# One inference step of a hybrid decoder layer on one core: the stages in front of the experts run once over all tokens, or twice over half of them each

## What is computed

```python
h   = x * (1 + sc_m) + sh_m                    # x is layernormed, sc/sh/gate from c @ w_ada
p   = h @ w_in                                 # 1024 -> 4608 columns
xs  = ps + (prev - ps) * mu_shift              # ps: the first 1792 columns, prev: the row before
r, k, v, decay, a, g = ...                     # from xs
y, wkv = _rwkv7_scan(r, decay, k, v, kk, a)    # state 64x64 per head, 8 heads, token after token
A   = (groupnorm(y) + bonus) * g
B   = window attention of q, k, v              # last 128 keys and the block's own, 8 heads, sinks
mix = (sigmoid(ga) * (A @ w_pa) + sigmoid(gb) * (B @ w_pb)) @ w_o
x   = LN(alpha * x + gt_m * mix)
ff  = PEER(x * (1 + sc_f) + sh_f)              # 8 heads, 2 x 128 keys, 16 of 16384 experts each
x   = LN(alpha * x + gt_f * ff)
```

## Time and profile before

| what | us |
|---|---|
| two runs | 4090.26, 4094.36 |
| median | 4092.31 |
| span of the profiled execution | 4092.5 |
| front, up to the experts | 1588 |
| peer_up | 1218 |
| peer_down | 1286.5 |
| TensorE busy | 3521.5 (86%) |
| VectorE busy | 2376.5 (58%) |
| GpSimd busy | 1416.8 (35%) |
| ScalarE busy | 1092.1 (27%) |

### The profile page before, as it was taken

How to read it: one execution, slowest core, us unless ns; L and a number is a source line. 1 busy time by engine, 2 the same in 40 slices (tenths; PEclk the granted TensorE clock), 3 DMA queues, 4 the chain that set the end, 5 groups by cost and what they waited for, 6 DMA issues and landing times. The chain is left out here.

```text
span 4092.5 us, 58784 instructions
## 1 busy us (share of the span) xinstructions
PE 3521.5 (86%) x22506; PEld 2542.8 (62%) x22506; DVE 2376.5 (58%) x4792; ACT 1092.1 (27%) x1919; POOL 1416.8 (35%) x1269
## 2 busy tenths in 40 slices
PE   6998999997879999988889989886787788778996
PEld 3666666673666888766666667664555455555565
DVE  3364222225223433999979888985666666665345
ACT  2221111111322232322262446343111111111122
POOL 0001111110002011344455545453666566665540
PEclk8999999997779999999999999998899899999998
DMA  5111110105123134788899999899999999999992
GB/s 196 36 31 38 33 33 29 37 28 202 67 84 148 42 101 140 247 291 282 302 389 348 338 355 380 328 338 353 391 390 382 363 394 397 394 395 396 393 350 76
DMA packets 367137, 973.75 MB, mean 238 GB/s; under 512 B 36017, under 2 KB 133497, under 8 KB 359952
## 3 DMA queue, kind: packets, MB, share of 16 engines
q0 software_dynamic: 150912, 549.52, 35.2%
q1 hardware_dynamic: 215952, 420.45, 29.1%
HBM read 863.29 MB, written 106.55 MB: 237 GB/s over the span
## 5 line engine op out<-in xcount | busy, mean ns | idle before, releaser
L2107 POOL DMA_INDIRECT u_rows<-in_u_rows,idx_u x512 | 640.5, 1251 | 859.1 <-DVE dots L2145 689.4
L2145 DVE CUSTOM_DVE_ANT_0 u_rows<-u_rows,x_rows 128x1024 f32<-128x1024 f32 x512 | 620.1, 1222 | 130.9 <-DMA u_rows<-in_u_rows,idx_u 110.0
L2118 POOL DMA_INDIRECT v_rows<-in_v,idx_v x512 | 590.2, 1153 | 258.0 <-issue 141.1
L2627 PE MATMUL hid_ps<-dh,u_high 128*128 128x512 f32 x1152 | 475.3, 413 | 84.9 <-DVE u_low L2884 62.2
L2627 PE MATMUL hid_ps<-dl,u_high 128*128 128x512 f32 x1152 | 472.0, 410 | 0.0
L2627 PE MATMUL hid_ps<-dh,u_low 128*128 128x512 f32 x1152 | 469.4, 407 | 0.0
L3084 ACT ACTIVATE dh<-v_raw 128x1024 fp32r<-128x1024 f32 x128 | 135.3, 1057 | 720.4 <-DMA v_raw<-in_v 549.7
L2627 PEld LDWEIGHTS hid_ps<-dh,u_high 128*128 128x128 f32 x1152 | 225.1, 195 | 151.4 <-DVE u_low L2884 84.3
L2204 PE MATMUL ff_ps<-v_rows,diag 128*8 128x512 f32 x2048 | 260.1, 627 | 65.2 <-DMA v_rows<-in_v,idx_v 63.6
L3139 PE MATMUL turn_ps<-w_high,dh 128*128 128x512 f32 x384 | 172.3, 449 | 150.1 <-DVEq L3221 125.1
L723 PE MATMUL side_ps_scan<-h,w_side_scan 128*128 128x344 f32 x768 | 269.7, 477 | 1.4 <-DMA w_side_scan<-in_w_side 1.2
(11 more groups left out here) (458 smaller groups left out, 6533.3 us busy)
## 6 DMA issues: line engine op xcount, KB each, us to landing
u_raw<-in_u SPq DMA_DIRECT2D x128, 512.0 KB
v_raw<-in_v SPq DMA_DIRECT2D x128, 512.0 KB, 12.3
hidden_saved<-hid SPq DMA_DIRECT2D x128, 256.0 KB, 6.6
gates_saved<-gates SPq DMA_DIRECT2D x32, 1024.0 KB, 8.0
hidden_back<-hidden_saved SPq DMA_DIRECT2D x128, 256.0 KB, 13.8
g_back<-gates_saved SPq DMA_DIRECT2D x64, 320.0 KB, 14.1
g_back<-gates_saved SPq DMA_DIRECT2D x32, 384.0 KB, 20.6
side_saved<-side_scan SPq DMA_DIRECT2D x16, 516.0 KB
```

The source lines that it names most:

```text
L2107: self.nc.gpsimd.indirect_dma_start(self.u[:, n % RU], None, self.io["u_rows"], bass.IndirectOffsetOnAxis(ap=index, axis=axis)).then_inc(l ...
L2118: self.nc.gpsimd.indirect_dma_start(self.v[:, n % RV], None, self.io["v"], bass.IndirectOffsetOnAxis(ap=index, axis=0)).then_inc(self.v_la ...
L2145: V.tensor_tensor_reduce(self.u[:, n % RU], self.u[:, n % RU], self.xt[:], 1.0, 0.0, ALU.mult, ALU.add, accum_out=self.dots[:, i % 2, k:k ...
L2627: mm = nc.tensor.matmul(ps[b % 2][:], u[:, b % RING, k], h[:, k], start=at == 0, stop=at == 3 * KD - 1)
```

## The change

The front is run twice. Part A holds prompt tokens 0 to 511 and the 8 samples (520 tokens, two tiles of 260 columns), part B tokens 512 to 1023 (one tile of 512). The row of stages is inputs, scan, group norm (with the samples in A), attention (with the samples' in A), merge and output for A, and then all of it for B; nothing of B stands beside A. What B needs of A is carried: the scan's state, the last projected row, and the last 128 keys and values. Weights (w_in, the side blocks, w_o, the merge's, the gate's) are loaded by each part. A scan has 8 chunks, an attention 4 blocks.

```diff
+class Part:
+    def __init__(self, tag, at, ns, before):
+        self.tag, self.at, self.ns, self.before = tag, at, ns, before
+        self.tp = TP // 2
+        self.t = self.tp + ns
+        self.nt = 2 if ns else 1
+        self.tn = self.t // self.nt
...
+PART_A = Part("a", 0, NS, None)
+PART_B = Part("b", TP // 2 + NS, 0, PART_A)
...
-                    rwkv_inputs(**env)
-                    rwkv_scan(**env)
-                    rwkv_samples(**env)
-                env["early"] = Early(nc, sems, mix)
-                attention(**env)
...
-                merge(**env)
...
-                output_and_queries(**env)
+                rwkv_inputs(**env, part=PART_A, h=ha, w=w, w_loaded=w_loaded, x_stored=x_stored)
+                rwkv_scan(**env, part=PART_A, h=ha)
+                rwkv_samples(**env, part=PART_A, x_at=x_at)
+            env["early"] = Early(nc, sb, sems, first, PART_A)
+            attention(**env, part=PART_A, x_at=x_at)
+            output_and_queries(**env, ha=ha, x_at=x_at)
...
+                    rwkv_inputs(**env, part=PART_B, h=hb, w=w, w_loaded=w_loaded, x_stored=None)
+                    rwkv_scan(**env, part=PART_B, h=hb)
+                    rwkv_samples(**env, part=PART_B)
+                env["early"] = Early(nc, sb, sems, second, PART_B)
+                attention(**env, part=PART_B)
+                output_dense(**env)
```

```diff
+    side_at = SIDE_SCAN if part.ns else 0
+    sides = SIDE - side_at
...
-                for n in range(3, COUNT + SIDE_MOVED):
+                if part.ns:
+                    sp.dma_start(before[:], io["shift_before"]).then_inc(small_loaded, 16)
+                else:
+                    for n in range(3):
+                        load(n)
...
+                for n in range(3, COUNT + sides):
                     load(n)
...
-        PAUSES = (3, 1, 4, 2, 2, 2, 2, 2, 2, 2, 2)
-        assert sum(PAUSES) == NT * KD
+        PAUSES = (4, 1, 3, 4, 4, 4, 4, 2, 2, 2, 2)
+        assert sum(PAUSES) == 2 * 2 * KD
```

```diff
-                low(0)
-                low(1)
-                for j in range(len(TILES)):
-                    for n in range(KD):
-                        join(j, n)
-                        if j == 0 and n + 2 < KD:
-                            low(n + 2)
-                        if j and n == 2:
-                            centre(j - 1)
...
-                        if j and n == 5:
-                            scale(j - 1)
+                for n in range(KD):
+                    o.join(dve, n)
+                o.centre(dve, 0)
+                o.centre(dve, 1)
+                o.scale(dve, 0)
+                o.scale(dve, 1)
```

```diff
-    out += [("rows", 0), ("split_u", 0), ("low_u", 0), ("scores", 0, 0), ("query", 0, 1), ("load_u", 2), ("split_u", 1), ("low_u", 1)]
+    out += [("rows", 0), ("split_u", 0), ("low_u", 0), ("scores", 0, 0), ("scores", 0, 1), ("query", 0, 1),
+            ("load_u", 2), ("split_u", 1), ("low_u", 1)]
...
-                out.append(("scores", m + 1, 0))
-                out.append(("query", m + 1, 1))
+                out += [("scores", m + 1, 0), ("scores", m + 1, 1), ("query", m + 1, 1)]
...
-                out.append(("scores", m + 1, 1))
+                out += [("scores", m + 1, 2), ("scores", m + 1, 3)]
```

More of the change, by code:

```diff
@@ L914, in step @@
                         return
[L915 removed]
+                    multiply(pe, n, 0)
                     for l in range(NL):
@@ L950, in step @@
                         S.activation(rhs, seq_ps[:, 0], ACT.Copy, scale=-1.0).then_inc(rhs_ready, 1)
-                    for t in takes(0) if n is not None else ():
-                        side.take(act, n, t)
+                    if n is not None:
+                        take(act, n, 0)
                     for l in range(NL):
@@ L1138, in _ @@
                 pe.wait_ge(g2_loaded, 16)
+                if not part.ns:
+                    for p in range(NP):
+                        variance(p)
+                    for p in range(0, NP, 2):
+                        back(p)
+                        back(p + 1)
+                        gate(p)
+                        gate(p + 1)
+                    return
                 ada.product(pe, 0)
```

2214 lines of the change are left out of this document (1185 added, 1029 removed).

## The result

The changed kernel takes 4316.5 us (4312.07 and 4320.94) against 4092.31 us: ratio 1.055, 95% interval 1.052 to 1.0581. The profiled execution spans 4310.3 us against 4092.5, so 217.8 us are to be found. The forecast was 4338.

The account below looks back on a forecast made before the run. It took almost every stage of the first 1588 us as bound by TensorE or a chain of dependent steps. Terms 168 - 42 + 22 + 12 - 10 + 9 + 68 + 19 = +246 us gave 4338 us, range 4224 to 4425.

Parts of the forecast that it names:

- Inputs: Input stages of both parts: more side blocks on TensorE, the bounding engine, and doubled edges; +168 us.
- Scan: Scan stages: A's chunks stay near before's, B's shorten without side work; -42 us.
- I expect both clocks in turn and take 28: B's scan: TensorE's clock alternates, so a chunk takes 28 us, between 22.3 at full clock and 34.6 at low.
- rival 1: B's scan and attention: the clock stays full, giving 4224 us; chance 0.12.
- Group norm and samples: Group norm and sample stage: a chain that mostly doesn't shrink with tokens, 80 us for A, 36 for B; +22 us.
- Attention: Attention: blocks of 21 us at low clock and doubled ends, +12 us; loads moved to the next stage, -10.
- Merge: Merge stage: same matmul time, edges paid twice; +9 us.
- Output: Output stage: layernorm chains with nothing beside them, 36 us in each part; +68 us.
- Experts: Expert stages: first weights loaded later, +6 us, and scores in quarters through one PSUM bank, +12.
- rival 3: peer_up: quartered scores hold TensorE and VectorE 8 us per selection, some 60 us more, 4398 us; chance 0.05.
- rival 2: B's scan, attention and bare layernorm chains: the clock is low throughout, giving 4409 us; chance 0.09.
- rival 4: B's inputs: side blocks are free because VectorE's chain holds the stage, giving 4141 us; chance 0.04.

Follow-up runs that it names:

- experiment 1: The changed kernel with part B's side blocks in the inputs making one of their eight products; 4214.99 us, one run.
- experiment 2: The changed kernel with 16 of part B's side blocks put back into B's scan, 6 left in its inputs; 4261.9 us, ratio 1.0421.
- experiment 12: The kernel before with its scan's loop written out, and extra unused matmuls at attention's start and in its first and last block; 4046.24 us, ratio 0.9874.
- experiment 4: The changed kernel with 16 extra unused matmuls at the start of each part's attention and 9 more per block; 4265.43 us, ratio 1.043.
- experiment 3: The changed kernel with 16 extra unused matmuls only at the start of each part's attention; 4298.06 us, one run.
- experiment 5: The kernel before with peer_up's scores in four quarters through one PSUM bank instead of two halves through two; 4121.69 us, ratio 1.0072.
- experiment 11: The changed kernel with 20 extra unused matmuls in front of the first chunk of B's scan; 4324.65 us, ratio 1.0551.
- experiment 10: The changed kernel with B's scan written as a loop of two chunks per turn; 4298.74 us, one run.

## Why the prediction was right, and by which steps

The direction, the range and, to 22 us, the size held. By step:

- **Inputs (+168; measured +187.5).** The mechanism held and experiment 1 confirms it: 36 blocks in B, one behind the other on TensorE. Mis-sized were the block, 7.40 us where I took 7.0 (0.10 more of matmuls, 0.30 of gap; 36 x 0.4 = 14), and A by 7.6, of which its blocks, some 7.2 us of matmuls as taken, had no share. TensorE was busy 90% of A's stage and 92% of B's, not over 95%.
- **Scan (-42; measured -90.3): the step that failed in size.** It is the term "I expect both clocks in turn and take 28". The chain was right: 22.3 worked out, 22.4 measured. What replaced the 28 is 23.5 on average ((1464.2 - 1299.5) / 7), since the low clock held for one chunk and a bit and not in each; that is 36 of the 48 us. So it is more than a size: the change between both clocks in each chunk did not come, and a chunk of B at 22 was the prediction's own sign for rival 1. A gives 14 more (and before's scan, 2 us shorter than the 559 I took, takes 2 off): I gave it before's 34.6 per chunk and it took 33.0. The sentence that the side work costs 12.1 of its 14.2 was a wrong reading too, and the level worked out beside it, where 2.4 us cost 1.25, spoke against it: 9.4 is side work, 2.7 the loop (experiments 2, 12). With 9.4 I would have seen that the move from the scan to the inputs loses a third of those 14.2 us and not a seventh; the sum for the place was still right, because chunk B left the loop as well.
- **Group norm and samples (+22; +10.8).** Inside the bounds (+6 to +38); B's share was 28.5, and A's 75.5, where I took 36 and 80.
- **Attention (+12 - 10; +8.0).** The block of 21 us at the low clock was right (20.7), and so was its cause, the clock lost in blocks with nothing beside them: experiment 4 takes some 50 us out by filling the pauses, and experiment 3 shows that a warm start is not enough. The loads in front of the merge gave 3.4 back, 15.4 against 18.82, not 10.
- **Merge (+9; +12.7).** By my cut 8.9 of the 12.7 are the wait in front of the product with w_o (7.10 and 9.10 us, before 7.32), which the forecast had in the output stage. The merge's own share is 3.8, less than the 9.
- **Output (+68; +56.0, or +64.9 with those 8.9).** The two chains were 71.8 for 72. A's stage was 203.7 for 205, but the terms that I wrote down for A (46, 8, 36 and 92 to 108) give 182 to 198 and not 205. Measured they are 49.3 for the products without their start, 34.1 for the chain, 110.6 for the queries and 9.8 of waiting for B's first weights, so this closeness is partly luck. B was 87.2 for 98: the products 46.3 for 45, their start of 8 stands in the merge's row, and the split came within the 37.7 of the chain instead of 9 behind it.
- **Experts (+18; +30.1).** The direction was right, the waits of rival 3 are real but half of what it gave: 51.0 us over 18 of them, of which peer_up pays 32.1. My 1 to 1.5 us per selection was too little: experiment 5 measured 30 / 9 = 3.3 us. The path was in the prediction, a quarter that waits for the copy of the one before it, which itself waits in ScalarE's order, up to 8.2 us; its price of 1 to 1.5 us was worked out from no row.

The misses of the scan (-48) and of the inputs and experts (+20, +12) lie on opposite sides; that the sum came within 22 us is partly luck. Rival 1 was half true: the clock stayed full in most of B's scan, and not in attention. Rivals 2 and 4 fell. Part of rival 3 came.

The Trainium skill ("TensorE: Matmul & The Clock Gate", "A second HAM failure mode: psum-queue depth-cycling") describes a kernel in which short idle times between groups of matmuls, not long waits, are enough to send the clock back and forth. Attention agrees in that short idle times were enough, 2.47 and 1.11 us in front of scores and values, and differs in that the clock did not go back and forth but stayed at 0.50 throughout.

## What to carry to other kernels

- Work that fills the pauses of a chain is not free there, but price it at each place by two runs: the same 14.2 us cost 9.4 in the scan and 14.8 in a stage of dense matmuls. Moving it to "somewhere else" is a loss as long as that place is bound by the same engine.
- Splitting a kernel by tokens keeps the matmul time and doubles what doesn't shrink: bare chains between stages (72 us here), the ends and starts, and the three attention blocks that lost their companion and with it the clock.
- A loop costs what its edges take and what the clock does behind them, and the price is not carried from one stage to another: 2.7 us per chunk of 34.4 in before's scan, 1.2 of 33.0 in A's, 0.9 of 23.4 in B's without side work. Writing out 14 chunks of before's scan paid 1%. And a second bank is worth more than the duration of the copy that empties it: the copy takes 0.6 us, and the 18 waits for it 2.8 us on average. What counts is how late that copy's engine may be.

## What the runs showed that I had not expected

- **TensorE's busy share does not tell the level of the clock.** In experiment 11 it was busy 17.56 of 24.00 us (73%) at 0.51 and then 45.10 of 62.00 (73%) at 1.00. The load was not the same: 258 records of matmuls in the first window are 11 per us, 1282 in the second 21. At the low clock the same work fills nearly twice the time (attention's values 7.09 us against 3.79), and so the engine looks busy.
- **The same instructions ran at either level.** The first chunk of B's scan, behind a wait of 8.8 to 9.1 us each time, took 28.6, 28.4 and 28.2 us at 0.56 in three kernels and 22.6 at 0.91 in two (experiment 10). A full clock at the start is not enough to keep it: behind the burst of experiment 11 it stayed for 6 us and fell. The Trainium skill ("TensorE: Matmul & The Clock Gate", "What's actually happening") says of a kernel's start that the number of slow matmuls differs between runs of one kernel; these rows show a difference of that kind inside a kernel, worth 6 us. What decides it stays open.
- **Matmuls that compute nothing can pay.** 9 of them per attention block, 4.7 us of TensorE by its records (3 took 1.56 us as six of them, the pairs 1.03), brought a block from 20.7 to 13.9 us.
- **A burst can come too late to help.** Idle time of TensorE in front of a stage can be its own sequencer's (6.88 us before the burst in experiment 11), and the burst placed there ran only behind it.
